# A layer's decayed recurrence by levels: pairs of levels on one key operand, with 192 query columns

## The chip, the core and the metric

The kernel runs on one of the eight cores of a Trainium2 chip. The measure is the device time of one execution in microseconds (us). The core has five engines that work side by side and wait for one another through semaphores: TensorE (PE, matmuls into PSUM banks `ps0` to `ps7`; its weight loads are listed as PEld), VectorE (DVE), ScalarE (ACT), GpSimd (POOL), and SyncE (SP), which here starts the DMAs of the weights.

## The reference

Two transformer-like layers of width 2048 over 256 tokens (plus 16 meta tokens in the first). The change touches one part of the first: the HGRN2 recurrence, 8 heads of 128 x 128, all in float32.

```python
def hgrn2_chunkwise(q, k, v, log_f):
    """S_t = diag(f_t) S_{t-1} + k_t v_t^T,  o_t = S_t^T q_t ; all float32."""
...
        b = jnp.cumsum(g_, axis=1)
        diff = b[:, :, None] - b[:, None, :]
        decay = jnp.exp(jnp.where(causal, diff, -jnp.inf))
        attn = jnp.einsum('bthd,bshd,btshd->bhts', q_, k_, decay)
        o_intra = jnp.einsum('bhts,bshv->bthv', attn, v_)
...
    qb = jax.nn.silu(q_b.astype(jnp.float32)).reshape(B, T, H_B, DK_B)
    f = lbh + (1.0 - lbh) * jax.nn.sigmoid(f_b.astype(jnp.float32).reshape(B, T, H_B, DK_B))
    o_b = hgrn2_chunkwise(qb, 1.0 - f, vb, jnp.log(f)).astype(x.dtype)
```

So `attn[t, s]` is a sum over the 128 features of query t times key s times the product of the forget factors between s and t, and it is needed for every s at or before t.

## The kernel before

The bulk of the program is weights. Every weight matrix comes from HBM as float32 in units of 1 MB (`raw`), is split into a rounded high part on ACT (`w_hi`, L835) and a rest on DVE (`w_lo = raw - w_hi`, L1368, 128x1024), and meets the activations in matmuls on PE. A chunk of 512 weight columns takes eight such splits and eight parts of PE's work; one of the eight is called a slot here. A slot has 24 matmuls with 272 moving columns where the chunk is made feature-major (L2314, then a group of eight in L2319), or 12 with 512 columns (L2304, L2305, then four in L2388). The last group of a slot waits for `w_lo`. `w_hi` and `w_lo` have four buffers each, so ACT's and DVE's splits run at most that far ahead of PE.

Every other piece of work of the layer is written into the slots by hand: each engine's code calls `branch_step(g)` behind slot g, and tables of slot numbers say what is issued there. An engine takes its instructions in this order, so a wait in a step holds up the next split or the next slot of that engine. The same slot number comes earlier in time on DVE than on PE, since DVE runs ahead with its splits.

`hgrn_step(g, half)` is the recurrence for four heads at a time (half 0 and 1), and `e` counts slots from its start `HG_AT[half]`. Within a block of 128 tokens (c = 0, 1) the pairs (s, t) are split into levels: level 0 is s = t, and level lev holds the pairs in which s lies in the first and t in the second half of one block of 2^lev tokens; LEVELS is 7. For each level

- DVE makes the queries of the later halves times the forget factors from the block's middle on (`ql`), and the keys of the earlier halves times the factors up to the middle (`kl`), with running products in `forget` and `back`, which are then doubled in reach (L1695, L1697);
- PE multiplies `kl` (128 stationary columns) by the later halves of `ql` (64 moving columns), 4 heads and 2 token blocks, 8 matmuls into `ps6` and `ps7` (L2597). A float32 matmul appears in the trace as two records, so this is a group x16. Level 0 is the same with 128 columns (L2601), and level 7 has only 64 key columns;
- DVE copies the results that a mask allows into `attn` (`copy_predicated`, L1664; level 0 in L1670), one instruction for each token block.

`level_ready` says that `ql` and `kl` are made, `level_prod` that the matmuls are done, `level_kept` that the copies are. `PITCH` gives the slots per level: 2 for half 0, whose slots are the feature-major ones, 3 for half 1. PE's level lev stands at e = 7 + (lev - 1) * PITCH and DVE's operands for it at the DVE slot e one higher. `link` marks an instruction on DVE behind which DVE waits for its own completion. The `ibt` rows are DVE's copies of the value projection out of PSUM (L1821) with PE's transpositions behind them (L2432, L2434). While half 0 runs, POOL computes features for the second layer.

`half_blocks(x, lev, which)` picks one half of each block:

```python
            n = 2 ** (lev - 1)
            if len(x.shape) == 3:
                return x.rearrange("p i (k s n) -> p i k s n", s=2, n=n)[:, :, :, which, :]
```

## Time and profile before

| | us |
|---|---|
| median of 3 runs | 2155.33 |
| lowest and highest | 2155.04, 2155.43 |
| the profiled execution | 2155.0 |
| its span in the profile | 2153.2 |
| PE busy | 2146.2 |
| DVE busy | 1380.5 |
| ACT busy | 1000.8 |
| POOL busy | 358.0 |

The span is cut from the first to the last recorded instruction; the rest of the execution's time, 1.8 us, lies around it. Busy times of different engines overlap. PE's records are pipelined, and their ends are modelled, so the length of a piece of PE's work is best read from start to start. The granted clock of PE is full in all 40 slices of the page. The recurrence stands at 360 to 460 us (half 0) and 475 to 600 us (half 1).

### The profile page before, as it was taken

Reading aid. Unit: us, or ns where it says so; the run is one execution under the profiler, and the core shown is the slowest. Engines: PE = TensorE matmul, PEld = TensorE weight load, DVE = VectorE, ACT = ScalarE, POOL = GpSimd, SP = SyncE. Lnnn points to the kernel's source line nnn. Section 1 sums busy time; section 2 is a strip of 40 time slices with the busy share of each in tenths; the row PEclk is TensorE's granted clock in tenths of the full one; section 3 lists DMA queues with packets and bytes.
Section 4 is the critical chain, followed back from the end, with each engine's and each line's share of the span. In section 5 each row is a group of like instructions: output and inputs, shape, how many; then the busy total and the mean of one; then the engine's idle time right before and its main releaser. Section 6 shows DMA issues by size and latency. Waiting matters only on the chain.

```text
span 2153.2 us, 34716 instructions
## 1 busy us (share of the span) xinstructions
PE 2146.2 (100%) x14296; PEld 1947.1 (90%) x14296; DVE 1380.5 (64%) x1876; ACT 1000.8 (46%) x1328; POOL 358.0 (17%) x437
## 2 busy tenths in 40 slices
PE   9999999999999999999999999999999999999999
PEld 7898889988888878899999999899999999998887
DVE  6778657968576576776786556556555555564444
ACT  6546544253354435555544445354444444444443
POOL 6563999770000000000000000000000000000000
PEclk9999999999999999999999999999999999999999
DMA  8655556445466644554456565555555555655553
GB/s 279 191 178 170 187 179 187 141 150 170 149 204 211 224 159 156 188 183 149 155 168 195 189 203 193 179 184 196 193 191 193 195 195 194 196 182 200 186 195 134
DMA packets 276531, 396.63 MB, mean 184 GB/s; under 512 B 9400, under 2 KB 198163, under 8 KB 270897
## 3 DMA queue, kind: packets, MB, share of 16 engines
q1 hardware_dynamic: 272704, 384.52, 54.2%
q0 software_dynamic: 3648, 10.37, 1.9%
q8 instruction: 81, 1.33, 0.2%
q14 instruction: 34, 0.27, 0.0%
q10 hardware_dynamic: 64, 0.14, 0.0%
HBM read 392.91 MB, written 2.10 MB: 183 GB/s over the span
## 4 chain that ended last, share of the span: by engine, by line
PE 97%; DVE 1%; DMA 0%; ACT 0%; issue 0%; SPq 0%; DVEq 0%
PE ps L2314 31%; PE ps L2319 16%; PE ps L2304 14%; PE ps L2305 14%; PE ps L2388 11%; PE ps L3011 4%; PE ps L2597 1%; PE ps L2347 0%; PE ps L2544 0%; DVE w_lo L1368 0%; DMA raw<-w_in 0%; PE ps L2504 0%; PE ps L2880 0%; PE ps L2820 0%; PE ps L2840 0%
## 5 line engine op out<-in xcount | busy, mean ns | idle before, releaser
L1368 DVE TENSOR_TENSOR w_lo<-raw,w_hi 128x1024 fp32r<-128x1024 f32 x719 | 897.2, 1255 | 592.7 <-ACT w_hi L835 586.8
L835 ACT ACTIVATE w_hi<-raw 128x1024 fp32r<-128x1024 f32 x719 | 752.4, 1058 | 696.5 <-PE ps L2319 418.2
L2314 PE MATMUL ps<-hf_hi,w_hi 128*128 128x256 f32 x1408 | 328.3, 276 | 0.0
L2314 PE MATMUL ps<-hf_lo,w_hi 128*128 128x256 f32 x1392 | 324.3, 276 | 0.0
L2314 PEld LDWEIGHTS ps<-hf_hi,w_hi 128*128 128x128 f32 x1408 | 264.3, 188 | 0.1
L2314 PEld LDWEIGHTS ps<-hf_lo,w_hi 128*128 128x128 f32 x1392 | 261.3, 188 | 0.0
L2304 PE MATMUL ps<-w_hi,h_hi 128*128 128x512 f32 x572 | 231.2, 404 | 0.7 <-DVE h_lo L1428 0.7
L2314 PE MATMUL ps<-x1t,w_hi 128*128 128x256 f32 x1680 | 228.2, 280 | 0.0
L2305 PE MATMUL ps<-w_hi,h_lo 128*128 128x512 f32 x572 | 223.5, 391 | 0.0
L2314 PEld LDWEIGHTS ps<-x1t,w_hi 128*128 128x128 f32 x1680 | 209.3, 188 | 1.4 <-issue 1.0
L2319 PE MATMUL ps<-hf_hi,w_lo 128*128 128x256 f32 x1408 | 188.2, 276 | 0.0
L2319 PEld LDWEIGHTS ps<-hf_hi,w_lo 128*128 128x128 f32 x1408 | 172.7, 188 | 0.0
L2388 PE MATMUL ps<-w_lo,h_hi 128*128 128x512 f32 x572 | 153.3, 390 | 0.0
L2304 PE MATMUL ps<-w_hi,st_hi 128*128 128x512 f32 x348 | 135.5, 389 | 0.0
L2305 PE MATMUL ps<-w_hi,st_lo 128*128 128x512 f32 x348 | 135.4, 389 | 0.0
L2388 PEld LDWEIGHTS ps<-w_lo,h_hi 128*128 128x128 f32 x572 | 107.4, 188 | 23.1
L2304 PEld LDWEIGHTS ps<-w_hi,h_hi 128*128 128x128 f32 x572 | 107.5, 188 | 21.9 <-DVE h_lo L1428 1.0
L2305 PEld LDWEIGHTS ps<-w_hi,h_lo 128*128 128x128 f32 x572 | 107.6, 188 | 20.7
L2319 PE MATMUL ps<-x1t,w_lo 128*128 128x256 f32 x896 | 120.5, 277 | 0.0
L2319 PEld LDWEIGHTS ps<-x1t,w_lo 128*128 128x128 f32 x896 | 110.5, 188 | 0.0
L2314 PE MATMUL ps<-h_hi,w_hi 128*128 128x272 f32 x384 | 98.8, 292 | 0.0
L2314 PE MATMUL ps<-h_lo,w_hi 128*128 128x272 f32 x384 | 96.7, 287 | 0.0
(523 smaller groups left out, 3168.4 us busy)
## 6 DMA issues: line engine op xcount, KB each, us to landing
raw<-w_in SPq DMA_DIRECT2D x163, 1024.0 KB, 5.1
raw<-w_ffn_gate SPq DMA_DIRECT2D x44, 1024.0 KB, 5.1
raw<-w_ffn_up SPq DMA_DIRECT2D x44, 1024.0 KB, 5.1
raw<-w_ffn_down SPq DMA_DIRECT2D x44, 1024.0 KB, 4.9
raw<-w_out SPq DMA_DIRECT2D x32, 1024.0 KB, 5.2
raw<-w_branch SPq DMA_DIRECT2D x16, 1024.0 KB, 5.2
raw<-w_br_hyena SPq DMA_DIRECT2D x8, 1024.0 KB, 5.7
raw<-w_br_attn SPq DMA_DIRECT2D x8, 1024.0 KB, 5.7
```

The lines of the kernel that those rows point to most:

```text
L835: act.activation(w_hi[:, h % 4, :, 0:width], raw[:, h // 2, 2 * (h % 2):2 * (h % 2) + 2, 0:width], ACT.Copy).then_inc(split_hi, 1)
L1368: dve.tensor_tensor(w_lo[:, h % 4, :, 0:width], raw[:, h // 2, 2 * (h % 2):2 * (h % 2) + 2, 0:width], w_hi[:, h % 4, :, 0:width].bitcast(F ...
L2304: pe.matmul(dst, left[0], w_h, start=first, stop=False)
L2305: pe.matmul(dst, left[1], w_h, start=False, stop=False)
L2314: pe.matmul(dsts[x], w_h, part, start=(k0 + e == 0 and i == 0), stop=False)
L2319: ins = pe.matmul(dsts[x], w_l, moving(k0 + e)[0], start=False, stop=(k0 + e == last))
L2388: ins = pe.matmul(dst, left(k, i)[0], w_lo[:, h % 4, e, 0:width], start=False, stop=(k == n - 1))
L2597: ins = pe.matmul(ps[6 + c][0:rows, i * (P // 2):(i + 1) * (P // 2)].rearrange("p (k n) -> p k n", n=2 ** (lev - 1)), kl[:, i, c * P:c * P ...
L3011: ins = pe.matmul(ps[bank][:, :], st_hi[:, par, s, cols], w_lo[:, h % 4, e, :], start=False, stop=last)
```

## The change

Levels 1 to 6 are taken as three pairs (1, 2), (3, 4), (5, 6). Both levels of a pair use one `kl`, the one of the lower level, for all keys (128x1024 instead of half of it). The queries of a pair lie side by side in `qm`, three groups of 64 columns per token block: the lower level's later halves, the upper level's later halves (`later`), and the same queries times the factors of one more quarter (`earlier`), which belong to the keys of the first quarter. PE then does one matmul with 192 moving columns for each head and token block: token block 0 at step 0 of a pair, token block 1 at step 2, and the bank is now chosen by heads (`ps6` for two heads, `ps7` for the other two). A pair has five steps (slots). On DVE `keep_pair` copies the three groups under masks, for two heads at a time: 6 copies of 128 elements for one token block. For the even levels the masks are told apart by quarters of a block. The work between a pair's operands is laid out over three DVE slots, where `forget` is doubled in parts.

Level 0 is copied at e = 8 (half 0) or e = 9 (half 1), level 7 stands alone behind the pairs. Half 0 takes 25 slots from `HG_AT` to `HG_END` instead of 22, half 1 26 instead of 29; what follows each, and half 1's start, move with them, and half 1 ends at the slot at which it ended. `kl`, `attn`, `state` and `kdm` have other addresses.

The core of the diff:

```diff
-        kl = at("kl", [P, 4, T], F32, g0 + 3 * 4352 + 2 * 4096)
-        attn = at("attn", [P, NT, 4, P], F32, g0 + 3 * 4352 + 3 * 4096)
-        state = at("state", [P, 4, P], F32, g0 + 3 * 4352 + 4 * 4096)
+        qm = at("qm", [P, 4, 3, T // 2], F32, g0 + 3 * 4352 + 4096)
+        kl = at("kl", [P, 4, T], F32, g0 + 3 * 4352 + 2 * 4096 + 2048)
+        attn = at("attn", [P, NT, 4, P], F32, g0 + 3 * 4352 + 3 * 4096 + 2048)
+        state = at("state", [P, 4, P], F32, d0 + 18 * KB)
         klm = at("klm", [P, 4, META], F32, g0 + 3 * 4352 + 4 * 4096 + 2048)
         kd = at("kd", [P, 4, P], F32, d0 + 16 * KB)
-        kdm = at("kdm", [META, 4, P], F32, d0 + 18 * KB)
+        kdm = at("kdm", [META, 4, P], F32, g0 + 3 * 4352 + 2 * 4096)
...
-        PITCH = [2, 3]
+        PAIRS, PAIR_STEPS, PAIR_AT = 3, 5, [8, 9]
...
-        HG_END = [HG_AT[0] + 8 + LEVELS * PITCH[0]]
+        HG_END = [HG_AT[0] + PAIR_AT[0] + PAIRS * PAIR_STEPS + 2]
         HG_AT.append(HG_END[0] + 8)
-        HG_END.append(HG_AT[1] + 8 + LEVELS * PITCH[1])
+        HG_END.append(HG_AT[1] + PAIR_AT[1] + PAIRS * PAIR_STEPS + 2)
...
+            def last_of(x4, lev, j, n=None):
+                n = n or 2 ** (lev - 1)
+                e = 2 ** (lev - 1)
+                return x4[:, :, :, j, e - 1:e].broadcast_to([P, 4, x4.shape[2], n])
+            def double_back(lev):
+                n = 2 ** (lev - 1)
+                lo = reach(lev)
+                f4 = forget[:, :, lo:TM].rearrange("p h (k s n) -> p h k s n", s=2, n=n)
+                b4 = back[:, :, lo:TM].rearrange("p h (k s n) -> p h k s n", s=2, n=n)
+                link(dve.tensor_tensor(b4[:, :, :, 0, :], b4[:, :, :, 0, :],
+                                       f4[:, :, :, 1, n - 1:n].broadcast_to([P, 4, (TM - lo) // (2 * n), n]), ALU.mult))
...
+            def double_forget(lev):
...
+                link(dve.tensor_tensor(f4[:, :, :, 1, :], f4[:, :, :, 1, :],
+                                       f4[:, :, :, 0, n - 1:n].broadcast_to([P, 4, (TM - lo) // (2 * n), n]), ALU.mult))
...
+            def first_of_pair(half, lev):
+                n = 2 ** (lev - 1)
+                dve.tensor_tensor(qm[:, :, 0, :].rearrange("p h (k n) -> p h k n", n=n), half_blocks(hq[:, :, :], lev),
+                                  half_blocks(forget[:, :, META:TM], lev), ALU.mult)
+                link(dve.tensor_tensor(kl[:, :, :], hkey[:, :, META:TM], back[:, :, META:TM], ALU.mult))
+            def second_of_pair(half, lev):
+                n = 2 ** (lev - 1)
+                double_back(lev)
+                f4 = quads(forget, lev)
+                link(dve.tensor_tensor(f4[:, :, :, 3, :], f4[:, :, :, 3, :], last_of(f4, lev, 2), ALU.mult))
+                later, earlier = (qm[:, :, j, :].rearrange("p h (k n) -> p h k n", n=2 * n) for j in (1, 2))
+                link(dve.tensor_tensor(later, half_blocks(hq[:, :, :], lev + 1),
+                                       half_blocks(forget[:, :, META:TM], lev + 1), ALU.mult))
+                t4 = forget[:, :, META:TM].rearrange("p h (k s n) -> p h k s n", s=4, n=n)
+                dve.tensor_tensor(earlier, later, last_of(t4, lev, 1, 2 * n), ALU.mult).then_inc(level_ready, 1)
+                dve.wait_ge(level_ready, (PAIRS + 1) * half + (lev + 1) // 2)
+            def keep_pair(half, p, c):
+                lev = 2 * p + 1
+                done = 2 * ((LEVELS + 1) * half + lev + c)
+                for b in range(2):
+                    dve.wait_ge(level_prod, done + b + 1)
+                    for j, (l, which) in enumerate(((lev, 1), (lev + 1, 1), (lev + 1, 0))):
+                        n = 2 ** (l - 1)
+                        src = ps[6 + b][:, 0:3 * P].rearrange("p (h j k n) -> p h j k n", h=2, j=3, n=n)[:, :, j, :, :]
+                        ins = dve.copy_predicated(half_blocks(attn[:, c, 2 * b:2 * b + 2, :], l),
+                                                  half_blocks(masks[:, l, :], l, which).unsqueeze(1).broadcast_to(
+                                                      [P, 2, P // 2 // n, n]), src)
+                        if j < 2:
+                            link(ins)
+                    ins.then_inc(level_kept, 1)
+                    dve.wait_ge(level_kept, done + b + 1)
...
-                lev, r = divmod(e - 8, pitch)
-                if e >= 8 and r == 0 and lev <= LEVELS:
...
+                p, r = divmod(e - PAIR_AT[half], PAIR_STEPS)
...
-                        dve.wait_ge(level_prod, 2 * (L0 + lev) + c + 1)
...
-                            ins = dve.copy_predicated(
-                                half_blocks(attn[0:rows, c, :, :], lev),
-                                half_blocks(masks[0:rows, lev, :], lev).unsqueeze(1).broadcast_to(
-                                    [rows, 4, P // 2 // n, n]),
-                                ps[6 + c][0:rows, 0:2 * P].rearrange("p (h k n) -> p h k n", h=4, n=n))
-                        else:
-                            ins = dve.copy_predicated(attn[:, c, :, :],
-                                                      masks[:, lev, :].unsqueeze(1).broadcast_to([P, 4, P]),
-                                                      ps[6 + c][:, :].rearrange("p (h n) -> p h n", n=P))
-                        ins.then_inc(level_kept, 1)
...
-                lev += 1
-                if e >= 8 and r == 0 and lev <= LEVELS:
-                    dve.tensor_tensor(half_blocks(ql[:, :, :], lev), half_blocks(hq[:, :, :], lev),
-                                      half_blocks(forget[:, :, META:TM], lev), ALU.mult)
-                    if lev == 1:
-                        ins = dve.tensor_tensor(kl[:, :, :], hkey[:, :, META:TM], back[:, :, META:TM], ALU.mult)
-                    else:
-                        ins = dve.tensor_tensor(half_blocks(kl[:, :, :], lev, 0), half_blocks(hkey[:, :, META:TM], lev, 0),
-                                                half_blocks(back[:, :, META:TM], lev, 0), ALU.mult)
-                    ins.then_inc(level_ready, 1)
-                    dve.wait_ge(level_ready, LEVELS * half + lev)
-                if e >= 8 and r == 1 and lev <= LEVELS:
...
-                    link(dve.tensor_tensor(b4[:, :, :, 0, :], b4[:, :, :, 0, :],
-                                           f4[:, :, :, 1, n - 1:n].broadcast_to([P, 4, kk, n]), ALU.mult))
-                    link(dve.tensor_tensor(f4[:, :, :, 1, :], f4[:, :, :, 1, :],
-                                           f4[:, :, :, 0, n - 1:n].broadcast_to([P, 4, kk, n]), ALU.mult))
...
+                if r == 0 and 1 <= p <= PAIRS:
+                    keep_pair(half, p - 1, 1)
+                if r == 0 and 0 <= p < PAIRS:
+                    first_of_pair(half, 2 * p + 1)
+                if r == 0 and p == PAIRS:
+                    dve.tensor_tensor(qm[:, :, 0, :].rearrange("p h (k n) -> p h k n", n=P // 2),
+                                      half_blocks(hq[:, :, :], LEVELS), half_blocks(forget[:, :, META:TM], LEVELS), ALU.mult)
+                    dve.tensor_tensor(half_blocks(kl[:, :, :], LEVELS, 0), half_blocks(hkey[:, :, META:TM], LEVELS, 0),
+                                      half_blocks(back[:, :, META:TM], LEVELS, 0), ALU.mult).then_inc(level_ready, 1)
+                    dve.wait_ge(level_ready, (PAIRS + 1) * (half + 1))
+                if r == 1 and 0 <= p < PAIRS:
+                    second_of_pair(half, 2 * p + 1)
+                if r == 1 and p == PAIRS:
+                    double_back(LEVELS)
+                    double_forget(LEVELS)
+                if r == 2 and 0 <= p < PAIRS:
+                    lev = 2 * p + 1
+                    f4 = quads(forget, lev)
+                    link(dve.tensor_tensor(f4[:, :, :, 1, :], f4[:, :, :, 1, :], last_of(f4, lev, 0), ALU.mult))
+                    double_back(lev + 1)
+                    double_forget(lev + 1)
+                if r == 3 and 0 <= p < PAIRS:
+                    keep_pair(half, p, 0)
+                if r == 2 and p == PAIRS:
...
+                        dve.copy_predicated(half_blocks(attn[0:n, c, :, :], LEVELS),
+                                            half_blocks(masks[0:n, LEVELS, :], LEVELS).unsqueeze(1).broadcast_to(
+                                                [n, 4, 1, n]),
+                                            ps[6 + c][0:n, 0:2 * P].rearrange("p (h k n) -> p h k n", h=4, n=n)
+                                            ).then_inc(level_kept, 1)
+                        dve.wait_ge(level_kept, 2 * (L0 + LEVELS) + c + 1)
...
-                lev = 0 if e == 6 else (e - 7) // pitch + 1
-                if e == 6 or (e >= 7 and (e - 7) % pitch == 0 and lev <= LEVELS):
-                    if lev:
-                        pe.wait_ge(level_ready, LEVELS * half + lev)
...
-                            cols = slice(c * P, (c + 1) * P)
-                            if lev:
-                                rows = P // 2 if lev == LEVELS else P
-                                ins = pe.matmul(ps[6 + c][0:rows, i * (P // 2):(i + 1) * (P // 2)].rearrange(
-                                    "p (k n) -> p k n", n=2 ** (lev - 1)), kl[:, i, c * P:c * P + rows],
-                                    half_blocks(ql[:, i, cols], lev), start=True, stop=True)
-                            else:
...
+                p, r = divmod(e - PAIR_AT[half], PAIR_STEPS)
+                if r in (0, 2) and 0 <= p < PAIRS:
+                    c = r // 2
+                    pe.wait_ge(level_ready, (PAIRS + 1) * half + p + 1)
+                    for b in range(2):
+                        pe.wait_ge(level_kept, 2 * (L0 + 2 * p + c) + b + 1)
+                        for x in range(2):
+                            i = 2 * b + x
+                            ins = pe.matmul(ps[6 + b][:, x * 3 * P // 2:(x + 1) * 3 * P // 2].rearrange(
+                                "p (j n) -> p j n", j=3), kl[:, i, c * P:(c + 1) * P],
+                                qm[:, i, :, c * (P // 2):(c + 1) * (P // 2)], start=True, stop=True)
+                        ins.then_inc(level_prod, 1)
+                if r == PAIR_STEPS - 1 and p == PAIRS - 1:
+                    n = P // 2
+                    pe.wait_ge(level_ready, (PAIRS + 1) * (half + 1))
+                    for c in range(NT):
+                        pe.wait_ge(level_kept, 2 * (L0 + LEVELS - 1) + c + 1)
+                        for i in range(4):
+                            ins = pe.matmul(ps[6 + c][0:n, i * n:(i + 1) * n], kl[:, i, c * P:c * P + n],
+                                            qm[:, i, 0, c * n:(c + 1) * n], start=True, stop=True)
...
+    for n in range(2, LEVELS, 2):
+        odd = (s >> (n - 2)) & 1 == 1
+        near = (s >> n == t >> n) & ((s >> (n - 1)) & 1 == 0)
+        m[n] = near & np.where((t >> (n - 1)) & 1 == 1, odd, ~odd)
```

DVE, from level 0 to the second level of half 0. In the kernel before, L1368 is a split, L1670 and L1664 are masked copies, L1678 and L1681 or L1683 make `ql` and `kl`:

```order
L1670 COPY_PREDICATED attn<-masks,ps 128x512 [waits level_prod,later_in]
L1670 COPY_PREDICATED attn<-masks,ps 128x512 [waits level_prod,level_kept]
L1678 TENSOR_TENSOR ql<-hq,forget 128x512 [waits level_kept]
L1681 TENSOR_TENSOR kl<-hkey,back 128x1024
L1368 TENSOR_TENSOR w_lo<-raw,w_hi 128x1024 [waits split_hi,level_ready]
L1695 TENSOR_TENSOR back<-back,forget 128x544
L1697 TENSOR_TENSOR forget<-forget 128x544 [waits dve_step]
L1368 TENSOR_TENSOR w_lo<-raw,w_hi 128x1024 [waits split_hi,dve_step]
L1664 COPY_PREDICATED attn<-masks,ps 128x256 [waits level_prod]
L1664 COPY_PREDICATED attn<-masks,ps 128x256 [waits level_prod,level_kept]
```

And in the changed kernel (splits are L1369 here, `qm` is L1663, L1674 and L1677):

```order
L1728 COPY_PREDICATED attn<-masks,ps 128x512 [waits level_prod,later_in]
L1728 COPY_PREDICATED attn<-masks,ps 128x512 [waits level_prod,level_kept]
L1663 TENSOR_TENSOR qm<-hq,forget 128x4x128 [waits level_kept]
L1665 TENSOR_TENSOR kl<-hkey,back 128x1024
L1369 TENSOR_TENSOR w_lo<-raw,w_hi 128x1024 [waits split_hi,dve_step]
L1649 TENSOR_TENSOR back<-back,forget 128x544
L1672 TENSOR_TENSOR forget<-forget 128x272 [waits dve_step]
L1674 TENSOR_TENSOR qm<-hq,forget 128x4x128 [waits dve_step]
L1677 TENSOR_TENSOR qm<-qm,forget 128x4x128 [waits dve_step]
L1369 TENSOR_TENSOR w_lo<-raw,w_hi 128x1024 [waits split_hi,level_ready]
L1749 TENSOR_TENSOR forget<-forget 128x272
L1649 TENSOR_TENSOR back<-back,forget 128x272x2 [waits dve_step]
```

The first level's operands were complete behind one product of `kl`; now a split, `back`, part of `forget` and two more `qm` come ahead of `level_ready`, and the next copies come behind another split.

PE, the end of the slot with the first level's matmuls, and what follows it. Before:

```order
L2314 MATMUL ps<-h_lo,w_hi 128x272
L2319 MATMUL ps<-h_hi,w_lo 128x272 [waits split_lo]
L2319 MATMUL ps<-h_hi,w_lo 128x272 x7
L2597 MATMUL ps<-ql,kl 128x64 [waits level_kept,level_ready]
L2597 MATMUL ps<-ql,kl 128x64 x3
L2597 MATMUL ps<-ql,kl 128x64 [waits level_kept]
L2597 MATMUL ps<-ql,kl 128x64 x3
L2314 MATMUL ps<-h_hi,w_hi 128x272 [waits split_hi]
```

In the changed kernel, one slot later:

```order
L2379 MATMUL ps<-h_lo,w_hi 128x272
L2384 MATMUL ps<-h_hi,w_lo 128x272 [waits split_lo]
L2384 MATMUL ps<-h_hi,w_lo 128x272 x7
L2663 MATMUL ps<-qm,kl 128x192 [waits level_kept,level_ready]
L2663 MATMUL ps<-qm,kl 128x192
L2663 MATMUL ps<-qm,kl 128x192 [waits level_kept]
L2663 MATMUL ps<-qm,kl 128x192
L2379 MATMUL ps<-h_hi,w_hi 128x272 [waits split_hi,fm_kept]
```

Two groups of four matmuls with 64 columns become two groups of two with 192, for one token block instead of two; the other token block follows two slots later.

## Rows read from the trace of the kernel before

**Rows 1.** The page, part 1: busy us (share of the span) and instructions of each engine.
```profile
PE 2146.2 (100%) x14296; PEld 1947.1 (90%) x14296; DVE 1380.5 (64%) x1876; ACT 1000.8 (46%) x1328; POOL 358.0 (17%) x437
```

**Rows 2.** Busy time by engine, 405 to 445 us; then clock, DMA share, GB/s.
```profile
core 0: us, PE busy (x) PEld busy (x) DVE busy (x) ACT busy (x) POOL busy (x), PEclk, DMA share, GB/s
...
405.00:445.00 40.00, 40.00 (x317) 38.18 (x315) 39.12 (x46) 11.38 (x20) 37.02 (x38) 1.00 0.46 147
```

**Rows 3.** Timeline of PE, first four heads: start us, length us, line, operation, count.
```profile
379.25 1.15 PE L2319 MATMUL ps<-h_hi,w_lo 128*128 128x272 f32 x8
...
384.00 1.15 PE L2319 MATMUL ps<-h_hi,w_lo 128*128 128x272 f32 x8
386.10 2.00 PE L2597 MATMUL ps<-ql,kl 128*128 128x64 f32 x16 [0.95 <-DVE kl L1681]
...
389.97 1.15 PE L2319 MATMUL ps<-h_hi,w_lo 128*128 128x272 f32 x8
...
392.93 1.15 PE L2319 MATMUL ps<-h_hi,w_lo 128*128 128x272 f32 x8
...
397.68 1.15 PE L2319 MATMUL ps<-h_hi,w_lo 128*128 128x272 f32 x8
...
408.36 1.15 PE L2319 MATMUL ps<-h_hi,w_lo 128*128 128x272 f32 x8
...
413.44 1.15 PE L2319 MATMUL ps<-h_hi,w_lo 128*128 128x272 f32 x8
```

**Rows 4.** Timeline of PE, second four heads.
```profile
494.61 1.07 PE L2388 MATMUL ps<-w_lo,h_hi 128*128 128x512 f32 x4
495.79 2.00 PE L2597 MATMUL ps<-ql,kl 128*128 128x64 f32 x16
...
504.96 1.07 PE L2388 MATMUL ps<-w_lo,h_hi 128*128 128x512 f32 x4
505.87 1.89 PE L2597 MATMUL ps<-ql,kl 128*128 128x64 f32 x16
...
509.50 1.07 PE L2388 MATMUL ps<-w_lo,h_hi 128*128 128x512 f32 x4
```

**Rows 5.** Timeline of PE, one insertion of four records with 256 columns.
```profile
945.07 1.07 PE L2319 MATMUL ps<-x1t,w_lo 128*128 128x256 f32 x8
...
948.67 1.07 PE L2319 MATMUL ps<-x1t,w_lo 128*128 128x256 f32 x8
...
951.39 1.07 PE L2319 MATMUL ps<-x1t,w_lo 128*128 128x256 f32 x8
```

**Rows 6.** Timeline of DVE, first four heads, levels 0 and 1.
```profile
382.40 1.52 DVE L1670 COPY_PREDICATED attn<-masks,ps 128x512 f32<-128x512 int32 x2
...
384.56 1.49 DVE L1681 TENSOR_TENSOR kl<-hkey,back 128x1024 f32<-128x1024 f32 x1
386.08 1.36 DVE L1368 TENSOR_TENSOR w_lo<-raw,w_hi 128x1024 fp32r<-128x1024 f32 x1
387.36 0.98 DVE L1695 TENSOR_TENSOR back<-back,forget 128x544 f32<-128x544 f32 x1
388.38 0.87 DVE L1697 TENSOR_TENSOR forget<-forget 128x544 f32<-128x544 f32 x1
```

**Rows 7.** DVE by line and form, 405 to 437.8 us: busy us, mean ns, idle before.
```profile
L1368 DVE TENSOR_TENSOR w_lo<-raw,w_hi 128x1024 fp32r<-128x1024 f32 x9 | 13.1, 1453 | 0.3
...
L1664 DVE COPY_PREDICATED attn<-masks,ps 128x256 f32<-128x256 int32 x8 | 3.5, 440 | 0.1
...
L1695 DVE TENSOR_TENSOR back<-back,forget 128x512 f32<-128x512 f32 x3 | 3.0, 1013 | 0.0
...
L1821 DVE TENSOR_TENSOR ibt<-ps,rsb 128x272 f32<-128x272 f32 x4 | 1.6, 430 | 0.1
```

**Rows 8.** Timeline of DVE, second four heads.
```profile
494.51 1.22 DVE L1681 TENSOR_TENSOR kl<-hkey,back 128x1024 f32<-128x1024 f32 x1
...
497.66 0.73 DVE L1697 TENSOR_TENSOR forget<-forget 128x544 f32<-128x544 f32 x1
...
500.70 1.51 DVE L1664 COPY_PREDICATED attn<-masks,ps 128x256 f32<-128x256 int32 x2
```

40 lines of the change are left out of this document (21 added, 19 removed).

## The prediction

> **What bounds the kernel now.** I read the page's busy line first. TensorE (PE) is busy 2146.2 of 2153.2 us [rows 1], so the time is the length of PE's stream: anything that lengthens or shortens that stream inside the recurrence moves the end one for one, and work on another engine counts only where PE waits for it. I then looked at the stretch where the recurrence runs. From 405 to 445 us (the first four heads) VectorE (DVE) is busy 39.12 of 40.00 us, GpSimd (POOL) 37.02, and PE all of it [rows 2]. So there are two engines at their limit there, and a change that gives PE less and DVE more has to be counted on both.
>
> PE's timeline gives the unit of the count. The projection goes in slots (an eighth of a chunk), each ending in one L2319 or L2388 group. Without an insertion a slot takes 392.93 - 389.97 = 2.96 us in the first four heads [rows 3], and 951.39 - 948.67 = 2.72 us for the slots that end in a 256-column x8 group; the 512-column slots in which the second four heads run have the same length to 0.01 us (504.96 to 509.50 is 4.54, which is 2.72 and a block of 1.82) [rows 4, 5]. A level's block of 16 records (8 float32 matmuls, two records each) lengthens a slot by 397.68 - 392.93 - 2.96 = 1.79 us; level 0, with 128 moving columns, by 384.00 - 379.25 - 2.96 = 1.79 us too [rows 3]. Half the columns at no gain: what costs there is loading the 128 stationary columns, 0.112 us a record. That is what the change goes for.
>
> PE also waits a little for DVE now. The first level's block starts at 386.10, though the slot's last group began at 384.00 and a block normally starts 0.99 us behind that: 1.1 us of waiting for `kl` [rows 3]. In the second four heads 495.79 - 494.61 = 1.18 where 0.91 is normal: 0.3 us [rows 4]. Later levels of the first four heads lose some 0.2 us more together (an estimate; the timeline shows starts a tenth late at two of them). Old waits: 1.6 us.
>
> **PE's part of the change.** Levels 1 to 6 were 12 blocks of 8 matmuls x 64 columns over both groups of heads. They become 12 blocks (3 pairs, 2 token blocks, 2 groups) of 4 matmuls x 192 columns, 8 records each. No float32 matmul with 192 columns is in the trace, so it is bounded by its neighbours: at 128 columns or fewer a record is 0.112 us, and four records with 256 columns (L2840) lengthen a slot by 948.67 - 945.07 - 2.72 = 0.88 us, 0.22 a record [rows 5]. 192 lies midway: 0.166, so 8 x 0.166 = 1.33 us a block (between 0.90 and 1.76). Saved: 12 x (1.79 - 1.33) = 5.5 us (between 0.4 and 10.7). Level 0 and level 7 are as before.
>
> **DVE's part.** Per pair of levels DVE had 8 products (two each of `ql`, `kl`, `back`, `forget`) and 4 predicated copies of 256 elements. Now it has 9 products (`qm` three times with 512, `kl` once with all 1024, `back` twice, `forget` as 272 + 272 + one whole) and 12 copies of 128 elements, each behind the one before through a semaphore. That is 512 more elements of products, 512 more of copies, and 9 more instructions. A copy of 512 elements takes 0.76 us (two in 1.52) [rows 6], one of 256 elements 0.44 us [rows 7], so one of 128 should take 0.44 - (0.76 - 0.44) / 2 = 0.28, and I add 0.03 for the chained wait: 0.31. Where the runs are one or two elements long (levels 1 and 2) 256 elements cost 0.755 [rows 8], which fits twice the time per element: 0.46 for 128. The bounds are 0.2 (no fixed part) and 0.5 (all fixed part, plus the wait).
>
> What these small copies cost is the point on which the trace of before is thinnest. The trace shows 0.44 us for the 128x256 copy out of PSUM. The Trainium skill, "VectorE: DVE Perf Modes", section on the TRN2 errata, says that VectorE pays a fixed latency per instruction, 120 cycles from PSUM at 0.96 GHz beside one cycle per element, and advises tiles of 512 elements and more; this speaks against cutting 4 copies into 12. By its row a 256-element copy would take 0.39 us and a 128-element one 0.26 us (an estimate from that page). The trace's 0.44 is higher than its 0.39, so I stay with my own price; with 0.26 each a pair would be 0.6 us cheaper and the total about 1 us lower.
>
> **Where it meets.** PE waits at the end of slot 8 + 5p for DVE's slot one further on, which now ends with `back`, part of `forget` and two products of `qm`. Counting for the first four heads:
>
> First wait. DVE reaches the end of `kl` at 386.05, splits weights until 387.36, does `back` until 388.38 [rows 6]; then 0.47 for half a `forget`, and 0.72 twice for the two `qm`: 390.3. PE, without the old wait, ends slot 8 at 384.98 + 2.96 = 387.94. It waits 2.4 us.
>
> From the first pair to the second, five slots. PE: 5 x 2.96 + 2 x 1.33 + 0.33 for one transposition group (413.44 - 408.36 - 2.96 - 1.79 [rows 3]) = 17.8. DVE: five splits at 1.25 = 6.25 (rows 6 has 1.28 from start to start, and POOL rests in part of it), one pair of `ibt` copies 0.8, three whole `back`/`forget` at 0.9 = 2.7, two halves 0.9, 12 copies at 0.46 = 5.5, `qm` 0.65, `kl` 1.4, two more `qm` 1.45: 19.7. DVE is longer, so PE waits 1.9 us.
>
> From the second to the third. PE: 14.8 + 2.66 + 0.66 = 18.1. DVE: splits 5 x 1.37 = 6.85, `ibt` twice 1.6, three at 1.01 = 3.05 [rows 7], halves 1.2, 12 copies at 0.31 = 3.7, `qm` 0.65, `kl` 1.5 [rows 6], `qm` twice 1.7: 20.25. PE waits 2.1 us. Behind the third pair DVE has only level 7, and PE's slots outrun nothing: no wait.
>
> Second four heads, where no operation is stretched (a whole `forget` is 0.73 instead of 1.01, `kl` 1.22 instead of 1.49 [rows 7, 8]). First wait: `kl` ended at 495.73 [rows 8]; now one split (1.15) comes ahead, one behind, and then 0.75 + 0.47 + 0.72 + 0.72: 500.7. PE's slot ends at 494.61 + 0.91 + 2 x 2.72 = 500.96: none. First to second pair: PE 5 x 2.72 + 2.66 = 16.3; DVE 5.75 + 2.25 + 0.95 + 5.5 + 0.6 + 1.25 + 1.45 = 17.75: PE waits 1.5. Second to third: the same with 3.7 for the copies is 15.95 against 16.3: none.
>
> New waits 2.4 + 1.9 + 2.1 + 1.5 = 7.9 us. They block nothing but PE's projection; what is queued behind them on PE is the next slot, for which DVE's weights lie ready. The three extra slots before the first group's end move its transpositions and copies to later slots with the same neighbours, at no cost. The moved tiles (`attn`, `kl`, `state`, `kdm`) keep their alignment to 256 bytes, and the mask table is as large as before: nothing.
>
> **Sum.** -5.5 (blocks) - 1.6 (old waits, replaced) + 7.9 (new waits) = +0.8 us. The profiled execution took 2155.0 us around its span of 2153.2, so it would become 2155.8; the median of the runs is 2155.33, so the forecast is 2156.1 us: PE's gain is given back as waits for DVE.
>
> **Rivals.**
> The copies decide against it (slower). If a copy of 128 elements costs 0.50 us, for its fixed part and its chained wait, second to third pair takes 12 x 0.19 = 2.3 us more with the first four heads, 15.95 + 2.3 - 16.3 = 1.9 more with the second, and the first pairs 0.5 more each: +5.2, 2161.3 us. It decides from about 0.45 us a copy. For it: 256 elements already cost 0.44, and six waits stand in each group. Against: the difference of 0.32 between 512 and 256 elements shows that elements do cost.
>
> DVE keeps up (faster). If the stretching of DVE by POOL falls elsewhere and the products run at their undisturbed times, both later waits of the first four heads and that of the second vanish and only the first, 2.4, stays: -5.5 - 1.6 + 2.4 = -4.7, 2150.6 us. For it: undisturbed, second to third pair is 15.95 + 1.6 = 17.5 against PE's 18.1. Against: POOL is busy 37.02 of 40.00 us there [rows 2] and its list is not changed.
>
> The wide matmul saves nothing. At 0.22 us a record a block is 1.76 and only 0.4 us is saved; PE's periods grow by 0.86, so the waits shrink by that to 2.4 + 1.0 + 1.2 + 0.6 = 5.2: -0.4 - 1.6 + 5.2 = +3.2, 2158.5 us. Against: at 128 columns a record still costs what the weight load does, so 192 can't well cost what 256 does.
>
> **Chances and range.** Forecast 0.58, copies decide 0.22, DVE keeps up 0.13, nothing saved 0.07. A difference below 0.2% (4.3 us, 2151.0 to 2159.6) is about what a measurement of this kernel can't tell from no change. Most of "keeps up" would come out only in part, so 0.08 for faster; the slow rival, with a little of the forecast's own spread, makes 0.24 for slower; 0.68 for the same. The range 2152.5 to 2161.5 takes in the slow rival's price and leaves out the full fast one; copies between 0.25 and 0.5 us and blocks between 1.2 and 1.5 us stay inside.
>
> **What would show it.** In the profile after: the x8 groups with 192 columns lengthening a slot by about 1.33 us; a wait of PE of about 2.4 us at 388, for `qm`; two of about 2 us near 408 and 428; one near 517, and DVE idle for almost nothing between 380 and 445. Copies of 128x128 elements at 0.46 us in the first pair and 0.3 in the others. The prediction is wrong if these copies take 0.45 or more, if DVE's products are not stretched as they are now, or if the wide record is far from 0.166 us.

## The result, and the profile after

The changed kernel takes 2163.95 us, the median of six runs (2162.62 to 2166.54); the kernel before, beside it on the same chip, 2155.28. The ratio is 1.0039, with a 95% interval of 1.0029 to 1.0049: 8.7 us slower, where 2156.1 was forecast and 2161.5 was the upper end of the range. The profiled execution took 2163.91 us around a span of 2162.1, so the two spans differ by 8.9 us.

The busy line of the page after, and from its part 4 the shares of the chain that ended last:

```profile
PE 2143.3 (99%) x14200; PEld 1943.5 (90%) x14200; DVE 1398.7 (65%) x1930; ACT 1000.7 (46%) x1328; POOL 358.9 (17%) x437
...
PE 94%; DVE 4%; issue 1%; ACT 0%; DMA 0%; SPq 0%; DVEq 0%
```

Against [rows 1] PE is busy 2.9 us less although the span is 8.9 us longer: PE is idle for 18.8 us in place of 7.0, some 12 us more, and of the 5.5 us that the blocks save its busy time shows only a part, since some matmuls ran at half clock (below). DVE has 54 instructions and 18 us more.

PE's timeline after (start us, length us, line, operation, count). L2384 and L2453 end a slot, L2663 are the blocks of a pair, L2673 is level 7's, and the brackets give the idle time before a row and who ended it:

```profile
387.19 1.15 PE L2384 MATMUL ps<-h_hi,w_lo 128*128 128x272 f32 x8
391.20 1.57 PE L2663 MATMUL ps<-qm,kl 128*128 128x192 f32 x8 [2.86 <-DVE qm L1677]
...
399.82 0.92 PE L2663 MATMUL ps<-qm,kl 128*128 128x192 f32 x4 [0.45 <-DVE attn L1689]
...
408.47 1.15 PE L2384 MATMUL ps<-h_hi,w_lo 128*128 128x272 f32 x8
...
412.79 1.66 PE L2663 MATMUL ps<-qm,kl 128*128 128x192 f32 x8 [2.84 <-DVE qm L1677]
...
417.74 1.16 PE L2384 MATMUL ps<-h_hi,w_lo 128*128 128x272 f32 x8
...
434.31 1.57 PE L2663 MATMUL ps<-qm,kl 128*128 128x192 f32 x8 [1.61 <-DVE qm L1677]
...
451.59 1.92 PE L2673 MATMUL ps<-qm,kl 128*64 128x64 f32 x16 [2.31 <-DVE kl L1738]
...
537.48 1.57 PE L2663 MATMUL ps<-qm,kl 128*128 128x192 f32 x8 [1.69 <-DVE qm L1677]
...
552.96 1.07 PE L2453 MATMUL ps<-w_lo,h_hi 128*128 128x512 f32 x4
553.87 1.46 PE L2663 MATMUL ps<-qm,kl 128*128 128x192 f32 x8
...
557.01 1.07 PE L2453 MATMUL ps<-w_lo,h_hi 128*128 128x512 f32 x4
```

The last three rows price a block that nothing disturbs: 557.01 - 552.96 - 2.72 = 1.33 us, the forecast value. The bracketed rows are the new waits. Counted from where the block should have started, 0.99 us behind the last L2384 (0.91 behind the last L2453, and 0.33 more where a transposition comes between), they are 3.0, 0.6, 3.0, 1.8, 2.5 and 1.9 us. Two of them were not in the sum at all: the 0.6 us for the first pair's copies at 399.82, and level 7's 2.5 at 451.59.

A second loss shows only in the clock. Four windows of the trace after, with the same columns as [rows 2]:

```profile
410.00:412.00 2.00, 0.00 (x0) 0.00 (x0) 1.93 (x3) 2.00 (x4) 1.88 (x2) 1.00 0.85 262
412.00:414.00 2.00, 1.21 (x7) 1.21 (x8) 1.97 (x2) 0.41 (x1) 1.84 (x3) 1.00 0.65 250
414.00:415.00 1.00, 1.00 (x7) 1.00 (x6) 1.00 (x3) 0.00 (x0) 1.00 (x1) 0.57 0.00 0
415.00:416.00 1.00, 1.00 (x6) 1.00 (x6) 0.97 (x4) 0.00 (x0) 0.92 (x2) 0.50 0.00 0
```

PE had stood for 2.84 us, and soon after it went on its granted clock fell to 0.50 (1.2 in place of 2.4 GHz) until 417.7. From 408.47 to 417.74 are 9.27 us, of which 2.96 is the slot, 1.33 the block and 0.33 a transposition; 4.65 are left, some 3.0 of waiting and 1.6 of slow clock. It falls again behind the 2.31 us at 451 (granted 0.50 from 452 to 455 us), which costs some 1.4 us. Taken as a sum: -5.5 - 1.6 + 12.8 (waits) + 3.1 (clock, an estimate from these slots) = +8.8, and the spans say +8.9. The experiments show that these terms can't be taken back one by one.

### The profile page after: what moved, and what is told of

Its sections match the earlier page's. It is cut to its first block, busy times and chain, and to the rows that moved or that the text cites. A ratio compares the mean times of both kernels' runs of the same rounds, so it can differ in the third digit from the quotient of the medians.

```text
span 2162.1 us, 34577 instructions
## 1 busy us (share of the span) xinstructions
PE 2143.3 (99%) x14200; PEld 1943.5 (90%) x14200; DVE 1398.7 (65%) x1930; ACT 1000.7 (46%) x1328; POOL 358.9 (17%) x437
## 4 chain that ended last, share of the span: by engine, by line
PE 94%; DVE 4%; issue 1%; ACT 0%; DMA 0%; SPq 0%; DVEq 0%
PE ps L2379 31%; PE ps L2384 15%; PE ps L2369 14%; PE ps L2370 14%; PE ps L2453 10%; PE ps L3082 4%; DVE w_lo L1369 1%; DVE attn L1689 1%; PE ps L2663 1%; PE ps L2412 0%; PE ps L2609 0%; DMA raw<-w_in 0%; PE ps L2569 0%; PE ps L2951 0%; PE ps L2891 0%
## 5 line engine op out<-in xcount | busy, mean ns | idle before, releaser
L1369 DVE TENSOR_TENSOR w_lo<-raw,w_hi 128x1024 fp32r<-128x1024 f32 x719 | 897.0, 1255 | 577.8 <-ACT w_hi L836 571.9
L2384 PE MATMUL ps<-hf_hi,w_lo 128*128 128x256 f32 x1408 | 188.2, 276 | 0.0
L2384 PEld LDWEIGHTS ps<-hf_hi,w_lo 128*128 128x128 f32 x1408 | 172.7, 188 | 0.0
L2453 PE MATMUL ps<-w_lo,h_hi 128*128 128x512 f32 x572 | 153.3, 390 | 0.0
L2453 PEld LDWEIGHTS ps<-w_lo,h_hi 128*128 128x128 f32 x572 | 107.4, 188 | 23.2
L2384 PE MATMUL ps<-x1t,w_lo 128*128 128x256 f32 x896 | 120.5, 277 | 0.0
L2384 PEld LDWEIGHTS ps<-x1t,w_lo 128*128 128x128 f32 x896 | 110.5, 188 | 0.0
```

Of the source, the lines that this page charges most:

```text
L1369: dve.tensor_tensor(w_lo[:, h % 4, :, 0:width], raw[:, h // 2, 2 * (h % 2):2 * (h % 2) + 2, 0:width], w_hi[:, h % 4, :, 0:width].bitcast(F ...
L2384: ins = pe.matmul(dsts[x], w_l, moving(k0 + e)[0], start=False, stop=(k0 + e == last))
L2453: ins = pe.matmul(dst, left(k, i)[0], w_lo[:, h % 4, e, 0:width], start=False, stop=(k == n - 1))
```

## The experiments

Theory A: DVE is the bound for the first four heads, and what PE loses is DVE's work less PE's. Rivals: the small copies alone; single orderings and the clock, each with a price of its own; GpSimd's stretching of DVE; and, after the sixth run, a burst that is badly placed.

**Level 7 a slot later, for the first four heads.**
```diff
-                if r == PAIR_STEPS - 1 and p == PAIRS - 1:
+                if e == PAIR_AT[half] + PAIRS * PAIR_STEPS - half:
```


> The changed kernel with one edit: in half 0 TensorE's level-7 matmuls stand one slot later (e = 23 in place of 22), so that VectorE has the slot of 2.9 us more to come to level 7's keys. Theory A (the level-7 wait is made by an ordering: VectorE stood 2.23 us at its second copy into ibt, which wants the transposition that TensorE issues at the end of slot 21, and then still had 6 copies and 2 products to do): the wait of 2.4 us goes, and with it the 1.5 us at half clock behind it, so 2164.0 - 3.9 = 2160.1 us, and the granted clock stays 1.00 between 448 and 460 us. Theory B (VectorE is simply late by its total work, so what waits is only moved to the end of the half, where TensorE waits for kd_ready): 2163 to 2165 us, with the idle time before L2682.

2163.20 us (2162.64 to 2164.33): of the 3.9 us that theory A gave, 0.75 came. Level 7's wait is gone; in PE's timeline there now stands, where `klm` is transposed at the end of these heads (0 idle in the changed kernel):

```profile
462.61 0.60 PE L2682 MATMUL ps<-ident,klm 128*16 128x128 f32 x4 [1.54 <-DVE ql L1769]
```

Theory B of that text holds for most of it: DVE's last product before that point starts at 461.1 here, at 460.0 in the changed kernel. PE may stop waiting for DVE early, but it then waits later.

**Work for PE inside two waits.**
```diff
+                if half == 0 and e in (13, 22):
+                    for _ in range(8):
+                        pe.matmul(ps[5][:, 0:P], ident[:, :], ident[:, :], start=True, stop=True)
```


> The changed kernel with one edit: ahead of the second pair's and of level 7's waits in half 0 (e = 13 and e = 22) TensorE makes 8 matmuls of 128 fp32 columns into a bank that nobody reads then (8 x 128 x 4 / 2.4 GHz, by the 1.33 us of 768 such columns 8 x 0.222 = 1.77 us), inside a wait of 3.0 and one of 2.4 us. Theory A (the granted clock fell to 0.50 because TensorE had stood for 2.9 and 2.3 us): the stand shortens to about 1.2 and 0.6 us, the clock stays 1.00, and the 1.6 + 1.5 us come back: 2164.0 - 3.1 = 2160.9 us. Theory B (the clock falls there whatever TensorE does, or the 3.1 us are no clock but a wait): 2164.0 us, within 0.5.

2163.97 us (2162.64 to 2164.42): nothing gained, nothing lost. PE's timeline, the filler and the second pair, then the third:

```profile
409.58 1.95 PE L2657 MATMUL ps<-ident 128*128 128x128 f32 x16
412.58 1.57 PE L2666 MATMUL ps<-qm,kl 128*128 128x192 f32 x8 [1.05 <-DVE qm L1677]
...
434.11 2.69 PE L2666 MATMUL ps<-qm,kl 128*128 128x192 f32 x8 [1.86 <-DVE qm L1677]
```

The stand shrank to 1.05 us and the clock stayed at 1.00 there and at level 7, as theory A of the text wanted. But the 1.6 us did not come back: the third pair starts at 434.11 (434.31 before the edit), since DVE is ready no sooner, and now it is behind that wait that the clock falls (the block lasts 2.69 us for 1.57; granted 0.60 from 434 to 436 us). So 3.5 us of extra matmuls, and a stretch at half clock, are free on PE while DVE is late. The clock is not free altogether: of the five executions the one with a mean granted clock of 1.000 took 2162.64 us, the three at 0.998 took 2163.97 to 2164.42. That is some 1.3 to 1.8 us, where the two falls had been put at 3.1.

**Without GpSimd beside it, both kernels.** GpSimd's operations behind its last rest (it stands from 394 to 404 us) are left out.
```diff
+                        if (g, 9 + 8 * k + n) < (8, 26):
                             link(pool.tensor_tensor(o, x, y, op))
```


> The changed kernel without GpSimd's products and sums from its last rest on (the feature sum of the second mixer's filter is left incomplete: 30 instructions of group 8 and groups 9 and 10 are left out, their loads stay). Theory A (VectorE is the bound in half 0, and it is late because GpSimd stretches its SBUF operations there, a product of 512 elements from 0.69 to 1.20 us): the waits of 3.0 us at the second pair and 1.85 us at the third go, with the 1.6 us at half clock; the first wait of 3.0 us, which lies ahead of GpSimd's start, stays, and about half of level 7's 3.9 us: 2164.0 - 3.0 - 1.6 - 1.85 - 1.9 = 2155.7 us. Theory B (the number and price of VectorE's own new operations make it late with or without GpSimd): at least the 3.0 and 1.85 us stay, 2162 us or more.

> The kernel before, with the same GpSimd work left out. Only 1.1 + 0.2 us of TensorE's waits lie in half 0 there: 2154.0 to 2155.3 us by both theories. It is the reference against which the run of the changed kernel without GpSimd is read.

The changed kernel falls to 2156.43 us (2156.28 to 2157.46), 7.5 us less; the kernel before stays at 2155.18 (2154.96 to 2155.75). PE's waits for the third pair and for level 7 in the changed kernel without GpSimd:

```profile
429.60 1.57 PE L2665 MATMUL ps<-qm,kl 128*128 128x192 f32 x8 [0.50 <-DVE qm L1679]
445.56 1.15 PE L2675 MATMUL ps<-qm,kl 128*64 128x64 f32 x16 [1.00 <-DVE kl L1740]
```

and two of DVE's forms there, 405 to 437.8 us (busy us, mean ns, idle before):

```profile
L1371 DVE TENSOR_TENSOR w_lo<-raw,w_hi 128x1024 fp32r<-128x1024 f32 x10 | 12.2, 1225 | 1.8 <-ACT w_hi L838 1.5
...
L1679 DVE TENSOR_TENSOR qm<-qm,forget 128x512 f32<-128x512 f32 x2 | 1.4, 692 | 0.1
```

With GpSimd the same view of the changed kernel has

```profile
L1369 DVE TENSOR_TENSOR w_lo<-raw,w_hi 128x1024 fp32r<-128x1024 f32 x7 | 10.5, 1507 | 0.4 <-ACT w_hi L836 0.2
...
L1677 DVE TENSOR_TENSOR qm<-qm,forget 128x512 f32<-128x512 f32 x2 | 2.0, 1013 | 0.1
```

The second pair no longer waits, the third only 0.50 us; the first wait, which lies ahead of what was left out, stays (2.49 us). So with these copies and products in place it is GpSimd's stretching that makes DVE late at the second and third pair; before the change the same stretching cost nothing measurable. The Trainium skill, "SBUF — State Buffer", section "SBUF: two separate sides", says that a VectorE operation with two SBUF inputs and a GpSimd operation that reads SBUF take one pair of ports in turn, each for its whole length. The rows agree in that products stretch from 692 to 1013 ns while copies out of PSUM do not (298 ns with GpSimd, 307 without).

**One copy instead of three.** For the first four heads the two copies of a pair's even level are left out.
```diff
+                        if half == 0 and j:
+                            continue
```


> The changed kernel with half 0's copies of a pair cut from three to one for each bank (the two copies of the even level are left out, so these scores stay zero). VectorE has 8 x 0.47 us less in the first pair and 8 x 0.33 us less in the others. Theory A (VectorE's sum of work is the bound in half 0): the waits at the second pair (3.0 us) and the third (1.85 us) go, with the 1.6 us at half clock, and level 7's wait of 2.4 us falls by the 4 copies of 0.33 us that stand ahead of it; the first wait of 3.0 us stays: 2164.0 - 6.5 - 1.3 = 2156.2 us, and 2154.7 us if the clock no longer falls at level 7. Theory B (TensorE waits for a chain, not for work: copies of one bank, product, matmul): the waits shorten by what stands directly ahead, 4 x 0.47 and 4 x 0.33 us, so 2164.0 - 1.9 - 1.3 = 2160.8 us or more.

2156.11 us (2154.97 to 2157.88), 7.8 us less for 8 x 0.47 + 16 x 0.33 = 9.0 us of copies: theory A's time to 0.1 us, and far from theory B's 2160.8. The waits agree less well, and part of the 0.1 us is luck: the second pair's is gone, but the third's is 0.85 and level 7's 0.23 us, the clock falls behind the first (the block lasts 2.93 us), and 0.76 us stand at `klm`. These waits are from the longest execution, of 2157.88 us. Either step, without GpSimd or with fewer copies, takes some 7.5 us away, so the lateness needs both the copies and GpSimd's stretching.

**Six slots for a pair.** For the first four heads; the second four start 5 slots behind their end, not 8.
```diff
-        PAIRS, PAIR_STEPS, PAIR_AT = 3, 5, [8, 9]
+        PAIRS, STEPS, PAIR_AT = 3, [6, 5], [8, 9]
...
-        HG_AT.append(HG_END[0] + 8)
+        HG_AT.append(HG_END[0] + 5)
```


> The changed kernel with 6 slots of TensorE for a pair in half 0 in place of 5; half 1 starts 5 slots behind the end of half 0 in place of 8, so at the same slot as in the changed kernel. Theory A (VectorE's sum of work against TensorE's slots): a pair in half 0 gets 2.96 us more, so the waits at the second pair (3.0 us, and 1.6 us at half clock) and at the third (1.85 us) go; level 7's 3.9 us go or fall to some 1 us since VectorE is no longer behind; the first 3.0 us stay: 2153.7 to 2156.5 us. Theory B (the lost time comes back where half 1 begins, whose first operations now stand closer behind the end of half 0): 2158 to 2162 us, with the waits between 475 and 500 us.

2164.02 us (2163.81 to 2165.38): no gain. PE still waits 2.89, 2.07, 0.74, 2.46 and 0.51 us in the first four heads. From their level 0 to that of the second four (L2652, the same number of slots) PE takes 127.6 us, where the changed kernel takes 128.8: 1.2 us less, where theory A gave 7.5 and more, so as I had put it it falls. The rest of the missing gain is in the second four heads, which start 5 slots behind the first and not 8: their first pair now waits 1.85 us and its block runs at low clock (2.61 us in place of 1.57), and from their level 0 to `klm` they take 69.6 us in place of 67.6. That is the theory B of the text in part, though its wait stands at 519 us and not before 500. (These times are from the longest execution, of 2165.38 us.) Why the first four heads gain so little, DVE's timeline between two of their pairs shows:

```profile
428.35 0.43 DVE L1886 TENSOR_TENSOR ibt<-ps,rsb 128x272 f32<-128x272 f32 x1
430.07 0.44 DVE L1886 TENSOR_TENSOR ibt<-ps,rsb 128x272 f32<-128x272 f32 x1 [1.29 <-PE ps L2499]
431.58 1.49 DVE L1369 TENSOR_TENSOR w_lo<-raw,w_hi 128x1024 fp32r<-128x1024 f32 x1 [1.07 <-ACT w_hi L836]
432.99 1.95 DVE L1689 COPY_PREDICATED attn<-masks,ps 128x128 f32<-128x128 int32 x6
...
440.83 0.82 DVE L1677 TENSOR_TENSOR qm<-qm,forget 128x512 f32<-128x512 f32 x1
```

DVE had time to spare and could not use it: it stands for a transposition of PE's and for `w_hi`, whose four buffers come free only as PE ends slots. From that split on come six copies, `qm`, `kl`, another split, `back`, part of `forget` and two more `qm` in a row, 10.1 us from 431.58 to 441.65; PE needs the end of it at 439.25, 7.7 us after its start, and waits the 2.46 us between. This reads as a burst against a bounded lead; the next run tests it.

**Six slots, and PE a slot later.** The same kernel with one more slot between DVE's products and PE's use of them.
```diff
-                p, r = divmod(e - PAIR_AT[half], STEPS[half])
+                p, r = divmod(e - PAIR_AT[half] - (1 - half), STEPS[half])
...
-                if r == 3 and 0 <= p < PAIRS:
+                if r == 4 - half and 0 <= p < PAIRS:
```


> The kernel with 6 slots for a pair in half 0, and TensorE's pair and level-7 matmuls one slot later there (slots 9 and 11 of the half, then 15 and 17, and so on; VectorE's copies of the first token block one slot later too). In the run with 6 slots alone TensorE still waited 2.89, 2.07, 0.74, 2.46 and 0.51 us in half 0, while VectorE itself stood 0.69, 1.29 and 1.07 us for ibt's transposition and for ScalarE's w_hi. Theory C (what is late is a burst: between a pair's last copies and its products VectorE has some 10 us of work, and it can't work ahead, since w_hi is a ring of four slots): one slot more between VectorE's products and TensorE's use of them takes up to 2.96 us from each wait, the first included: 2155 to 2158 us. Theory A (only the sum of VectorE's work against the number of slots counts, wherever it stands): no change against 2164.0 us by more than 1 us.

2158.44 us (2157.42 to 2159.49), ratio to before 1.0014 (1.0005 to 1.0023) against 1.0038 (1.0024 to 1.0052): 5.6 us less with the same instructions. Theory A, no change by more than 1 us, is out; theory C holds in the main, at 0.4 us outside its figure. From level 0 to level 0 the first four heads take 121.0 us in place of 127.6. The waits for `qm` at the first and third pair and level 7's are gone, but the second pair's is not shorter (2.18 us), and 1.5 us stand for copies; in the second four heads there are two (1.86 and 1.70 us), the first of which the changed kernel does not have, with its start 8 slots behind; they take 69.6 us again.

**More work for DVE, both kernels.** Three harmless operations of 512 elements.
```diff
+                if half == 0 and e in (10, 15, 20):
+                    link(dve.tensor_tensor(back[:, 0:2, META:TM], back[:, 0:2, META:TM], back[:, 0:2, META:TM], ALU.max))
```


> The changed kernel with three more operations on VectorE in half 0, one in each pair (the maximum of 512 elements of back with themselves, which changes nothing; 0.69 us undisturbed, up to 1.2 beside GpSimd). Theory A (VectorE is the bound throughout half 0, with nothing to spare): the time grows by their whole length, 3 x 0.69 to 3 x 1.2: 2166.1 to 2167.6 us. Theory B (TensorE's waits have other causes, and VectorE has room between them): under 2165.0 us.

> The kernel before with the same three operations at the same slots (10, 15 and 20 of half 0). VectorE was busy 39.12 of 40.00 us there and TensorE hardly waited. If VectorE's lead over TensorE (it may run up to four slots ahead) takes them up: 2155.3 to 2155.9 us. If before was already at VectorE's limit in half 0, they show whole: 2157.4 us or more, and then each microsecond that the change adds to VectorE there costs one.

The three take 3.1 us in the changed kernel and 2.9 in the kernel before. The first goes from 2163.95 to 2165.02 us (2164.15 to 2165.38), less than theory A gave and at the upper edge of theory B; the second from 2155.23 to 2156.62 (2156.11 to 2160.29, four of eleven at 2159.6 or more, their mean granted clock 0.998 and that of the others 1.000), between its two figures: more than if its lead hid them, and less than their whole length. Up to the third pair they pass through nearly whole in the changed kernel (its block starts at 436.26 in place of 434.31, for 2.2 us of extra work by then); at level 7, DVE's stand for PE's transposition takes 0.9 us of it up (1.37 in place of 2.23). And the kernel before had room for about half of such work on DVE, not more.

**Pairs for the second four heads only.** The first four run by single levels as before. To read one table of masks, a pair's even level is copied whole, then its odd quarters over it.
```diff
-        m[n] = near & np.where((t >> (n - 1)) & 1 == 1, odd, ~odd)
+        m[n] = near & np.where((t >> (n - 1)) & 1 == 1, True, odd)
```


> Half 0 by single levels as in the kernel before, half 1 by pairs as in the changed kernel (the masks are put so that both read one table: a pair's even level is copied whole first, then its odd quarters over it). The 6 blocks of half 1 save 6 x 0.46 = 2.8 us and the old wait of 0.3 us goes; the new wait between first and second pair of half 1 costs 1.97 + 0.2 us as it did in the changed kernel. Theory A (the loss is half 0's alone): 2155.3 - 2.8 - 0.3 + 2.2 = 2154.4 us. Rival (the changed addresses, masks or half 1 carry part of the loss): 2157 us or more.

> As the kernel with pairs in half 1 alone, but with 6 slots for a pair there. The wait of 1.97 us between the pairs goes, since VectorE gets 2.72 us more for a pair: 2155.3 - 2.8 - 0.3 = 2152.2 us, faster than both kernels. Rival (the work that the three more slots push towards the next stage is late there): 2155 us or more.

With 5 slots 2154.67 us (2154.3 to 2157.11), ratio 0.9998 (0.9989 to 1.0007); with 6 slots 2153.01 (2152.71 to 2155.26), ratio 0.9990 (0.9981 to 0.9999). The second is the fastest kernel of the study, 2.3 us under the kernel before (2155.31 beside it), where 2152.2 was expected. PE's records of level 0 and of the end of the second four heads, in the kernel with 6 slots:

```profile
491.33 1.95 PE L2720 MATMUL ps<-hq,hkey 128*128 128x128 f32 x16
...
565.48 0.60 PE L2750 MATMUL ps<-ident,klm 128*16 128x128 f32 x4
```

and in the kernel before:

```profile
491.00 1.95 PE L2601 MATMUL ps<-hq,hkey 128*128 128x128 f32 x16
...
567.93 0.60 PE L2611 MATMUL ps<-ident,klm 128*16 128x128 f32 x4
```

74.15 against 76.93 us over the same number of slots: 2.78 saved, of 2.8 forecast for the blocks (6 x 0.46) and 0.3 for the old wait. So the wide matmul gives what the sum said, but for 0.3 us, where DVE can keep up; GpSimd is idle there.

**The old wait as well.** That kernel, with everything of the first four heads from level 1's matmuls on a slot later.
```diff
-                    lev = 0 if e == 6 else (e - 7) // PITCH + 1
+                    lev = 0 if e == 6 else (e - 8) // PITCH + 1
```


> The kernel with pairs in half 1 alone and 6 slots for each, and in half 0, by single levels, everything from level 1's matmuls on one slot later (level 1's keys stay where they are). It takes the wait of 1.1 us that the kernel before has at level 1's keys: 2153.0 - 1.1 = 2151.9 us. Rival (the later end of half 0 makes half 1's first steps late, or the wait comes back at level 2): 2153.0 us.

2153.40 us (2153.02 to 2153.93): no gain. The 0.95 us of standing at level 1 is gone, and 0.70 and 0.29 us stand at two later levels (413.17 and 421.77 us): the rival's case, though at later levels than it named.

## Why the prediction was wrong

The forecast was 0.8 us over before; the spans say 8.9. The term that failed is that of the new waits, +7.9 us: it came to 12.8 us, and the slow clock behind two of them, 3.1 us, had no term. None of the three signs that the prediction named for being wrong came (the copies were 0.33 and, as forecast, 0.47 in the first pair; products were stretched, more than priced; the wide record was 0.166 us), and no rival names what happened. By its steps:

1. **The blocks, -5.5 us: right.** 1.33 us a block, the middle between two neighbours, and 2.78 us saved in the second four heads with six of them, the old wait of 0.3 us included.
2. **The old waits, -1.6: right**, none is left.
3. **The copies: right.** 0.31 and 0.46 us were priced; six take 1.95 to 2.00 us, and 2.83 to 2.87 in the first pair, so 0.33 and 0.47. The rival of 0.50 us falls, though its time of 2161.3 was nearer.
4. **First wait, 2.4: 3.0.** The `forget` of 272 elements took 0.80 us, not 0.47, and the two `qm` 0.83 each, not 0.72. Some 0.2 us of the `forget` is its own: it takes 0.68 where GpSimd is idle. No run takes the rest, which lies beside GpSimd (busy 1.76 of 2.00 us from 388 to 390), away.
5. **First to second pair: DVE 19.7, was 21.6.** The failed term is the price of products beside GpSimd. The forms of DVE from 391.05 to 412.75 us (busy, mean ns):

```profile
L1369 DVE TENSOR_TENSOR w_lo<-raw,w_hi 128x1024 fp32r<-128x1024 f32 x5 | 6.3, 1280 | 0.1
L1689 DVE COPY_PREDICATED attn<-masks,ps 128x128 f32<-128x128 int32 x12 | 5.4, 446 | 0.3
...
L1674 DVE TENSOR_TENSOR qm<-hq,forget 128x512 f32<-128x512 f32 x1 | 1.2, 1200 | 0.0
L1663 DVE TENSOR_TENSOR qm<-hq,forget 128x512 f32<-128x512 f32 x1 | 1.0, 970 | 0.0
L1749 DVE TENSOR_TENSOR forget<-forget 128x272 f32<-128x272 f32 x1 | 0.9, 919 | 0.0
...
L1672 DVE TENSOR_TENSOR forget<-forget 128x272 f32<-128x272 f32 x1 | 0.6, 578 | 0.0
```

   Splits and copies are as forecast (6.25 and 5.5). The two halves of `forget` are 1.5 in place of 0.9, the first `qm` 0.97 for 0.65, the later two 1.20 each (L1674 above, and L1677 from 411.53 us) for 0.725: together the missing 1.9 us. Of the 0.6 us of the `forget`, some 0.2 are again the first pair's pattern (0.66 us in the second four heads) and not stretching. PE's own 17.8 us held, so it lost 3.8 and not 1.9: 3.0 us for `qm`, and 0.6 to 0.7 for the copies at 399.82, on which the prediction had no wait.

6. **Second to third pair: DVE 20.25, was 21.5**, mostly splits (1.56 us each for 1.37). PE's visible wait was 1.8 for 2.1 forecast, an agreement by luck: 1.6 us of PE's half clock stand in the place of waiting.
7. **"Behind the third pair DVE has only level 7 ... no wait": wrong, and the dearest single step (2.5 us of waiting and 1.4 of slow clock, for nothing forecast).** From the end of the third pair's `qm` DVE took 17.3 us until it had level 7's products, with this in the middle:

```profile
443.90 0.43 DVE L1886 TENSOR_TENSOR ibt<-ps,rsb 128x272 f32<-128x272 f32 x1
446.55 0.44 DVE L1886 TENSOR_TENSOR ibt<-ps,rsb 128x272 f32<-128x272 f32 x1 [2.23 <-PE ps L2499]
446.91 2.00 DVE L1689 COPY_PREDICATED attn<-masks,ps 128x128 f32<-128x128 int32 x6
448.94 1.36 DVE L1736 TENSOR_TENSOR qm<-hq,forget 128x512 f32<-128x512 f32 x1
450.22 1.31 DVE L1738 TENSOR_TENSOR kl<-hkey,back 128x512 f32<-128x512 f32 x1
```

DVE stands for PE's transposition, and only then may it do 4.7 us of work that PE waits for a slot later. PE's block was due 14.8 us behind the third pair's. I had neither added up DVE's work there (some 15 us without the stand) nor seen who holds DVE up, nor that the copies, now in a group of six, stand ahead of the products. Moving PE's use a slot later took the wait away but not the time (0.75 us), so the price of this step by itself is not shown. Without GpSimd 1.0 of the 2.3 us are still there, with a third of the copies 0.2.

8. **The clock: no term, 3.1 us seen.** Moving level 7 gave back 0.75 of its wait and slow clock together, and filling the waits nothing in the median.
9. **Second four heads, 1.5: 1.9.** The mechanism was right.

Steps 5 and 6 compared sums over five slots, and with the measured durations these sums come out (21.6 against 17.8 us): there the prices failed. The wait at the copies and step 7 can't be read from such a sum at all. [rows 2] had DVE busy 39.12 of 40.00 us, and the kernel before turned 2.9 us of extra work into 1.4 us of time, so there was little slack to average over; and the six-slot runs show that where the work stands counts as much (5.6 us) as how much it is.

## What to carry to other kernels

Where a second engine is at 98% beside the one that bounds, price what a change adds to it with the longest duration that the trace shows for that form beside the third engine, and follow its order up to each point where it is waited for, with the waits that hold it itself; a sum over a period gives only the lower end. A wait or a slow clock that shows on the waiting engine need not be worth its length (a wait of 2.3 us with its slow clock gave back 0.75 here): put work into it, and if the time stays, go to the engine that is late. And try such a trade where the helper is free: the same matmuls gave their 2.8 us with the second four heads.
